# Attention with two heads in the two row halves of the matmul array, in units of a head pair and a query tile

## The reference

```python
def gqa_attend(q, k, v):
    s = einsum('bkgqd,bksd->bkgqs', q, k) * (HEAD_DIM ** -0.5)      # 1/8
    p = softmax(s, axis=-1)
    return einsum('bkgqs,bksd->bkgqd', p, v)
# latent queries (256) attend to context + latent keys (512); context queries (256) to context keys (256)
# q, k: RMS-normed over the 64 channels, the latent ones rotated; then y = o @ w_o for both streams
```

## Time and profile before

| what | value |
|---|---|
| time of three runs | 3343.28, 3342.68, 3339.27 us; median 3342.68 |
| profiled execution, span from first to last instruction | 3341.7 us (the profile gives no other time of that execution) |
| busy: TensorE matmul / weight loads | 3125.3 us (94%) / 2416.2 us (72%) |
| busy: VectorE / ScalarE / GpSimd | 1803.7 (54%) / 708.2 (21%) / 38.0 us (1%) |
| TensorE's mean granted clock | 0.973 |
| projections of the attention | about 2075 to 2160 us of the span |
| its units | 2160 to 2282 us |

### The profile page before, as it was taken

How to read it: one execution, slowest core, us unless ns; L and a number is a source line. 1 busy time by engine, 2 the same in 40 slices (tenths; PEclk the granted TensorE clock), 3 DMA queues, 4 the chain that set the end, 5 groups by cost and what they waited for, 6 DMA issues and landing times.

```text
span 3341.7 us, 50848 instructions
## 1 busy us (share of the span) xinstructions
PE 3125.3 (94%) x21694; PEld 2416.2 (72%) x21694; DVE 1803.7 (54%) x2751; ACT 708.2 (21%) x1342; POOL 38.0 (1%) x76
## 2 busy tenths in 40 slices
PE   8999988999998999999889998988999999998998
PEld 8987764558976997765457984544788886465797
DVE  5554554556555555454565555574434562287565
ACT  1112213212112102222311103261211001244110
POOL 1000000000000000000000000000000000000000
PEclk9999999999999999999999999999999999998999
DMA  8654402226655755321215743200223343231352
GB/s 272 227 173 140 164 28 76 76 76 218 213 185 184 252 172 173 128 88 65 88 51 183 236 150 132 76 1 26 76 76 101 114 163 107 77 125 58 127 177 101
DMA packets 279696, 430.75 MB, mean 129 GB/s; under 512 B 9880, under 2 KB 147456, under 8 KB 279472
## 3 DMA queue, kind: packets, MB, share of 16 engines
q1 hardware_dynamic: 273920, 411.52, 36.4%
q0 software_dynamic: 5088, 14.86, 1.4%
q10 hardware_dynamic: 464, 1.12, 0.1%
HBM read 426.43 MB, written 1.05 MB: 128 GB/s over the span
## 4 chain that ended last, share of the span: by engine, by line
PE 82%; DVE 11%; ACT 4%; issue 2%; DMA 1%; DVEq 0%; ACTq 0%; POOL 0%; SPq 0%; PEldq 0%
PE bank L446 80%; PE bank L449 2%; DVE arena L742 1%; ACT xT L993 1%; DVE arena L3700 1%; DVE arena L3621 1%; DVE arena L1761 1%; ACT xT L2810 1%; ACT arena L3137 0%; DMA ring<-in_ffn_w 0%; DVE stats L916 0%; DVE ctok L1773 0%; DMA ring<-in_ple_w_gate 0%; DVE arena L3268 0%; DVE ring L742 0%
## 5 line engine op out<-in xcount | busy, mean ns | idle before, releaser
L446 PE MATMUL bank<-arena 128*128 128x128 f32 (+8 forms) x7068 | 786.7, 286 | 49.9 <-DVEq L3704 8.4
L446 PE MATMUL bank<-xT,ring 128*128 128x128 f32 (+3 forms) x4640 | 808.5, 335 | 20.5 <-ACTq L2818 9.9
L446 PEld LDWEIGHTS bank<-arena 128*128 128x128 f32 (+3 forms) x7068 | 667.7, 164 | 165.9 <-issue 27.0
L446 PEld LDWEIGHTS bank<-xT,ring 128*128 128x128 f32 (+1 forms) x4640 | 691.9, 194 | 130.7 <-issue 55.0
L446 PE MATMUL bank<-ring,xT 128*128 128x512 f32 (+2 forms) x1408 | 592.2, 572 | 17.0 <-ACT xT L2810 8.7
L446 PEld LDWEIGHTS bank<-ring,xT 128*128 128x128 f32 x1408 | 261.2, 194 | 287.6 <-issue 268.7
L446 PE MATMUL bank<-ring,arena 128*128 128x256 f32 (+1 forms) x1584 | 448.5, 436 | 19.7 <-DVE arena L839 6.5
L446 PEld LDWEIGHTS bank<-ring,arena 128*128 128x128 f32 x1584 | 302.8, 193 | 140.2 <-issue 91.0
L782 DVE TENSOR_TENSOR arena<-arena,bank 128x256 f32<-128x256 f32 (+1 forms) x198 | 92.2, 466 | 427.1 <-PE bank L446 287.2
L694 ACT COPY arena<-bank 128x256 f32<-128x256 f32 (+1 forms) x264 | 107.8, 408 | 777.5 <-PE bank L446 776.5
L742 DVE TENSOR_TENSOR arena<-ring,arena 128x1024 f32<-128x1024 f32 (+1 forms) x216 | 257.1, 1190 | 7.4
(11 more groups left out here) (391 smaller groups left out, 2140.1 us busy)
## 6 DMA issues: line engine op xcount, KB each, us to landing
ring<-in_ffn_w SPq DMA_DIRECT2D x88, 1024.0 KB, 8.0
ring<-in_w_in SPq DMA_DIRECT2D x32, 2048.0 KB, 7.7
ring<-in_ffn_w_in SPq DMA_DIRECT2D x44, 1024.0 KB, 6.9
arena<-in_ada_w SPq DMA_DIRECT2D x18, 2048.0 KB, 13.6
ring<-in_ffn_w SPq DMA_DIRECT2D x16, 2048.0 KB, 7.9
ring<-in_ffn_w_out SPq DMA_DIRECT2D x12, 2048.0 KB, 8.2
ring<-in_hgrn_w_in SPq DMA_DIRECT2D x12, 2048.0 KB, 7.9
ring<-in_ffn_w SPq DMA_DIRECT2D x8, 1536.0 KB, 6.6
```

The source lines that it names most:

```text
L446: return self.e.matmul(o, lhsT, rhs, start=start, stop=stop, skip_group_check=True)
```

## The change

- Keys are kept once, as `kk` (each key head written twice side by side, one copy with a broadcast source) and `kT`, 4 x 512 columns instead of 8 x 512; there is no zeroed buffer. The upper and the lower 64 partitions of a column of `kT` hold the same key head. A tile's keys need four transposes and one copy.
- A score product runs over 64 partitions: `qT[r_, ...]` and `kT[r_, ...]` with `r_` the upper or lower half. The even head goes through the upper half of the array's rows into one bank, the odd head through the lower half into the next bank.
- A unit is a head pair and a query tile in the latent stream (16 units), and a head pair with both query tiles in the context stream (8 units).
- The banks of the units are fixed: scores in banks 4 and 5 or 6 and 7 by the unit's parity (`score_pair`), turned probabilities in 2 and 3 (`turn_pair`), weighed values in 0 or 1. All eight banks are now one tensor, so that one instruction can read two. New semaphores count units: scores_ready, scores_read, probs_turned, values_weighed, values_kept.
- A unit has one maximum over both banks (1024 columns) and one product with -0.125. The scalings of a unit are issued without a wait between them. The second copy of turned probabilities is VectorE's in the context stream.
- The order is TensorE scores(u), turn_probs(u-2), weigh(u-3); ScalarE keep_PT(u-2), exps(u); VectorE maxes(u), scale(u-1), keep_PT(u-2) (context), keep_o for unit u-4.

```diff
-        kz = t(8, P)
-        kTz = t(8, 512)
+        kk = t(4, P)
+        kT = t(4, 512)
...
-                for src in (qk_tok[:, QKV_ORDER[n - 1]], kz[:].rearrange("p a b -> p (a b)")):
-                    for q in range(2):
+                for src, nq in ((qk_tok[:, QKV_ORDER[n - 1]], 2), (kk[:].rearrange("p a b -> p (a b)"), 1)):
+                    for q in range(nq):
...
+            pe.wait_ge(to_act.freed, to_act.next_free() + 3)
+            pe.wait_ge(to_dve.freed, to_dve.next_free() + 3)
             def scores(u):
...
+                i, s, qt = units[u]
+                if u >= 2:
+                    pe.wait_ge(scores_read, u - 1)
+                for q in (qt,) if s == 0 else range(2):
+                    for par, r_ in enumerate(CHUNKS):
+                        bank = score_pair(u)[:, par]
+                        o = bank if s == 0 else bank[:, q * SEQ:(q + 1) * SEQ]
+                        mm = pe.mm(o, qT[r_, i, s * SEQ + q * P:s * SEQ + (q + 1) * P], kT[r_, i // 2, s * SEQ:512])
+                mm.then_inc(scores_ready, 1)
             def turn_probs(u):
...
+                pe.wait_ge(probs_scaled, u + 1)
+                if u:
+                    pe.wait_ge(PT_ready, 2 * u)
+                for par in range(2):
+                    for k in range(4):
+                        o = k * P if s == 0 else k % 2 * SEQ + k // 2 * P
+                        mm = pe.turn(turn_pair[:, par, k * P:(k + 1) * P], Pb[:, u % 2, par, o:o + P])
+                    mm.then_inc(probs_turned, 1)
+            def weigh(u):
+                n = 8 * s + i
+                bank = psum[n % 2]
+                pe.wait_ge(PT_ready, 2 * u + 2)
+                if n >= 2 and qt == 0:
+                    pe.wait_ge(values_kept, n - 1)
+                nk, w = (4, P) if s == 0 else (2, SEQ)
+                for k in range(nk):
+                    for par, r_ in enumerate(CHUNKS):
+                        mm = pe.mm(bank[r_, qt * P:qt * P + w], av_tok[:, 2 * s + k, g_], PT[:, u % 4, par, k * w:(k + 1) * w],
+                                   k == 0, k == nk - 1)
+                if s or qt:
+                    mm.then_inc(values_weighed, 1)
+            for u in range(len(units) + 3):
+                if u < len(units):
                     scores(u)
+                if 2 <= u < len(units) + 2:
+                    turn_probs(u - 2)
+                if u >= 3:
+                    weigh(u - 3)
...
         def attention_units():
-            return [(h, s) for s in range(2) for h in range(16)]
+            return [(i, 0, qt) for i in range(8) for qt in range(2)] + [(i, 1, 0) for i in range(8)]
...
             def exps(u):
+                if u >= 2:
+                    act.wait_ge(probs_turned, 2 * u - 2)
+                act.wait_ge(scores_ready, u + 1)
+                act.wait_ge(max_ready, act.due(max_ready))
+                for j in range(2 if s == 0 else 4):
+                    ins = e.activation(probs(u, j), src, ACT.Exp, scale=0.125, bias=bias[:, j:j + 1],
+                                       accum_out=total[:, j:j + 1])
...
+                ins.then_inc(scores_read, act.up(scores_read))
             def keep_PT(u):
+                for par in range(2 if units[u][1] == 0 else 1):
+                    act.wait_ge(probs_turned, 2 * u + par + 1)
+                    ins = e.copy(PT[:, u % 4, par], turn_pair[:, par])
...
+            for u in range(len(units) + 2):
+                if u >= 2:
+                    keep_PT(u - 2)
                 if u < len(units):
                     exps(u)
...
-            v.memset(kz[:], 0.0).then_inc(dve_step, dve.up(dve_step))
...
+                ins = v.tensor_copy(kk[:].rearrange("p g (r n) -> p g r n", r=2),
+                                    x[:, 16:20].unsqueeze(2).broadcast_to([P, 4, 2, 64]))
...
             def maxes(u):
+                dve.wait_ge(scores_ready, u + 1)
+                src = score_pair(u)
+                if units[u][1]:
+                    src = src.rearrange("p r (q n) -> p r q n", q=2)
+                ins = v.tensor_reduce(by_query(u, am[:, 16:24]), src, AX.X, ALU.max)
...
             def scale(u):
+                v.reciprocal(r, by_query(u, am[:, 8:16])).then_inc(dve_step, dve.up(dve_step))
+                dve.wait_ge(dve_step, dve.sent(dve_step))
+                for j in range(n):
+                    ins = v.tensor_scalar(probs(u, j), probs(u, j), r[:, j:j + 1], None, ALU.mult)
...
+            for u in range(len(units) + 4):
+                if u < len(units):
+                    maxes(u)
+                if 1 <= u <= len(units):
+                    scale(u - 1)
+                if u >= 2 and u - 2 < len(units) and units[u - 2][1]:
+                    keep_PT(u - 2)
+                if u >= 4:
+                    i, s, qt = units[u - 4]
+                    if s or qt:
+                        keep_o(8 * s + i)
```

More of the change, by code:

```diff
@@ L283, in two_blocks @@
         block_landed = [sem(f"block_landed{i}") for i in range(RING)]
-        psum = [ctx.enter_context(nc.psum_tensor(f"bank{i}", [P, 512], F32)) for i in range(8)]
+        bank_all = ctx.enter_context(nc.psum_tensor("bank", [P, 8, 512], F32))
+        psum = [bank_all[:, i] for i in range(8)]
         to_dve = Banks(psum[:4], dve_bank_filled, dve_bank_freed)
@@ L3029, in turn_probs @@
-            def turn_probs(u):
[L3030 to L3050, removed]
-                for k in range(nk):
[L3052 to L3056, removed]
@@ L3095, in act_attention @@
                     t0 = QKV_ORDER[n - 1] * P
-                    for dst in (qT, kTz):
-                        for q in range(2):
+                    for dst, nq in ((qT, 2), (kT, 1)):
+                        for q in range(nq):
                             act.wait_ge(to_act.filled, to_act.next_filled())
@@ L3118, in exps @@
             def exps(u):
[L3119 to L3144, removed]
-                            ins.then_inc(act_step, act.up(act_step))
-                            act.wait_ge(act_step, act.sent(act_step))
-                    act.sem_inc(probs_ready, act.up(probs_ready))
@@ L3149, in keep_PT @@
-            def keep_PT(u):
-                h, s = units[u]
-                for k0 in range(0, 4 if s == 0 else 2, 2):
-                    act.wait_ge(to_act.filled, to_act.next_filled())
-                    bank = to_act.filled_bank()
-                    ins = e.copy(PT[:, u % 4, k0:k0 + 2], bank[:].rearrange("p (k t) -> p k t", k=2))
-                    ins.then_inc(to_act.freed, act.up(to_act.freed))
-                    act.wait_ge(to_act.freed, act.sent(to_act.freed))
-                act.sem_inc(PT_ready, act.up(PT_ready))
@@ L3276, in keep_o @@
-            def keep_o(u):
-                h, s = units[u]
-                dve.wait_ge(to_dve.filled, to_dve.next_filled())
-                bank = to_dve.filled_bank()
-                ins = v.tensor_copy(oT[:, h // 2, s * SEQ:(s + 1) * SEQ], bank[:, 0:SEQ])
-                ins.then_inc(to_dve.freed, dve.up(to_dve.freed))
-                dve.wait_ge(to_dve.freed, dve.sent(to_dve.freed))
-            for u in range(len(units) + 3):
+                dve.wait_ge(scores_ready, u + 1)
+                src = score_pair(u)
@@ new lines, in scale @@
+            def scale(u):
+                r = by_query(u, am[:, 24:32])
+                dve.wait_ge(probs_ready, dve.due(probs_ready))
+                v.reciprocal(r, by_query(u, am[:, 8:16])).then_inc(dve_step, dve.up(dve_step))
+                dve.wait_ge(dve_step, dve.sent(dve_step))
+                n = 2 if units[u][1] == 0 else 4
+                for j in range(n):
+                    ins = v.tensor_scalar(probs(u, j), probs(u, j), r[:, j:j + 1], None, ALU.mult)
+                    done = probs_scaled if j == n - 1 else dve_step
+                    ins.then_inc(done, dve.up(done))
+                dve.wait_ge(dve_step, dve.sent(dve_step))
+                dve.wait_ge(probs_scaled, dve.sent(probs_scaled))
@@ L3285, in dve_attention @@
+            for u in range(len(units) + 4):
                 if u < len(units):
                     maxes(u)
-                if u >= 4 and u % 2 == 0:
-                    keep_o(u - 4)
-                if u < len(units):
-                    scale(u)
+                if 1 <= u <= len(units):
[6 more added lines that the diff above has]
+                        keep_o(8 * s + i)
```

120 lines of the change are left out of this document (46 added, 74 removed).

## The result

The changed kernel takes 3306.4 us (median of 4 runs) beside 3341.3 for the kernel before: ratio 0.9891, interval 0.9877 to 0.9905, 34.8 us less. In two later groups of runs it was 3313.3 (ratio 0.9920, 0.9903 to 0.9937) and 3308.0 (0.9900, 0.9883 to 0.9916). Beside the kernel before in the same groups that is 27.1 and 31.5 less, so the total tells the gain to some 8 us only, and what follows rests on the traces. I forecast 3313, some 30 less, with 3309 to 3317 as the forecast's own range.

The account below looks back on a forecast made before the run. TensorE was taken to bound the latent stream, VectorE the context stream. Projections -1.9 and attention -28.0 gave -29.9 us from 3342.68: 3312.8, forecast 3313, own range 3309 to 3317, wider range 3306 to 3325.

Parts of the forecast that it names:

- the wide one: Range of the total that leaves out rivals D, E and the edges: 3306 to 3325 us.
- Projections: Before the attention: 16 fewer key transposes and one fewer last copy on ScalarE, together -1.9 us.
- S: Score products of a latent unit on TensorE: 1.28 us, between 0.86 (full overlap) and 1.71 (none).
- Three slots, 1.28: Latent scores: in-order queue lets only second half A run beside first half B, so 1.28 us a unit.
- rival B: Latent scores overlap fully: S 0.86, a unit 3.07, -5 us, total 3308; chance 0.10.
- W: Weighing in a latent unit on TensorE: 16 instructions of 128 columns, 0.90 us.
- the changes of shape: TensorE's tile-shape switches in a latent unit: two more visible ones at 0.15 us each, between 0 and 0.24.
- T: Transposes in a latent unit on TensorE: eight, 1.01 us, unchanged in number.
- Start: Start of attention: table load under the first maximum, T0 at 6.2 us, 1.5 added for a lower clock.
- Context stream: Eight attention units bound by VectorE at 4.34 us each; entry 16.5, three periods 13.0, tail 9.8.
- Behind it: Output projection after attention: starts at the low clock before and after, weights no new wait; nothing added to the sum.
- Rival D: TensorE's clock stays at 1.2 GHz in the attention stage: latent +38 us, context +15, total 3366; chance 0.04.

Follow-up runs that it names:

- the one with zeros: Changed kernel's units, banks and order, but keys with zeros beside them and score products over all 128 rows: 3321.8 us, ratio 0.9942.
- the halves alone: Kernel before, its units, banks and order kept, but keys kept once and score products over 64 rows: 3347.7 us against 3339.7, ratio 1.0021.
- the two maxima: Changed kernel with two maxima of 512 columns a unit instead of one of 1024: 3310.0 us, ratio 0.9911.
- one unit ahead: Changed kernel, but transposes of unit u-1, weighing of u-2, and VectorE's scaling in the round of its maximum: 3352.5 us, ratio 1.0032.
- both products in one half: Changed kernel with both score products of a unit in the upper row half, the even head's computed twice: 3324.6 us, ratio 0.9955.

## Where the prediction was right, and where it failed

The direction, the stage and the engines that bound it held. The first group's 3306.4 lies below the forecast's own range of 3309 to 3317 and at the lower edge of the wide one. By the profiled spans the gain was 4.9 us larger than forecast: 4.4 from the latent rounds, 2.3 behind the stage and 0.7 ahead of the attention, less 1.5 in the context stream and 1.0 in the rest. The other two groups' gains, 27.1 and 31.5, lie on both sides of the 29.9; that these come nearer says nothing for the sum, since the stage in their traces, 91.9 and 91.6, is within 1 us of the first one's.

- **Projections**: -1.9 forecast. The trace has -2.6 up to the first scores, of which 0.7 was there before the first attention transposes (2080.68 before, 2079.98 after); -1.9 is left. The stretch from those transposes to the first scores repeats: 79.4 in the kernel before and in the one with zeros, 77.4 in all three profiles of the changed kernel and with the halves alone.
- **The step that failed is S.** I wrote "Three slots, 1.28". It measured 0.86: rival B, to which I gave 0.10, was the case, and with it 3308 against 3306.4 measured. The first context scores come 50.1 us after the first scores (first row below), where I had 54.5; the twelve rounds before them take 3.12 on average instead of 3.50, and that is the 4.4. The argument for three slots was an in-order queue that no row of the trace had shown; one product half beside the next, and even one after four of the other, overlap in full. The burst on 64 x 64 tiles already ran near the full four-fold rate (1.10 us with its tail, where the columns need 0.86), and I should have given it more weight. The section of the Trainium skill that I had set beside the rows (TensorE: Matmul & The Clock Gate, "Measured speedup vs the span model") says that packed tiles finish in about one matmul. The trace agrees with that rule: 0.86 and not 1.28.

```profile
2207.57 0.73 PEld L452 LDWEIGHTS bank<-arena 64*128 64x128 f32 x8 [0.17 <-issue]
...
2224.87 1.23 DVE L3234 TENSOR_REDUCE arena<-bank 128x4 f32<-128x1024 f32 x1
...
2237.49 1.22 DVE L3234 TENSOR_REDUCE arena<-bank 128x4 f32<-128x1024 f32 x1
...
2244.03 1.06 PE L455 MATMUL bank<-cst,arena 128*128 128x128 f32 x8 [0.67 <-DVEq L3258]
...
2246.61 1.08 PE L452 MATMUL bank<-arena 128*64 128x256 f32 x8 [0.50 <-DVE arena L3262]
```

- **ScalarE** was sized at 2.95 a latent unit and measures 3.19: the two copies take 1.28 together, and 0.20 passes between a copy and the next exp. With TensorE down to 3.10, that became the bound of the last units, so a little of S's error was given back.
- **W** (0.90) and the changes of shape (0.15 each): T, W and S with all switches were to be 3.49; with S at 0.86 that is 3.07, and 3.10 was measured.
- **Start**: the table load does not lie under the first maximum; the load waits until the maximum is there (2160.18), and the first transposes came at 6.9 instead of 6.2. The clock of a stretch of 6 us there was 0.72, as in the kernel before.
- **Context stream**: period 4.34 forecast, 4.20 measured, because the four scalings without waits take 1.14 (1.23 to the next instruction) and not 1.45. Its entry and tail were mis-sized the other way. By the rows above, the entry to the fifth maximum took 17.3 (16.5 forecast), three periods 12.6 (13.0) and the tail 10.9 (9.8): 1.5 longer in all. In the tail I had left out that the last transposes wait for VectorE's copy of turned probabilities of the unit before, and the last weighing for its copy of weighed values (last two rows). VectorE as bound is confirmed by the two maxima (+0.19 a unit gave +0.20) and by moving work away from it.
- **Behind it** I had put nothing, since I took the projection to start at the low clock before and after. It starts at 0.65 in the one profile of the kernel before and at full clock in every profile of this document's other kernels, with the halves alone too, in the old units and order. So the -2.3 is measured, but that the change brings it is not shown.
- **Rival D** did not happen in this kernel, but its mechanism is real and fits what makes the halves alone slower than before. I had argued against it from a burst of half-array products without a wait, and from waits between full-array products; the case that counts has both.

Left open: why the changed kernel's single runs spread from 3300.6 to 3322.0, when those of the kernel before spread from 3335.1 to 3344.6. In the one profile at 3322 the stage is as in the others (91.6), and most of the loss lies in the recurrent layer some 650 us later, whose code is the same: that profile lags the first one by 2.7 us where the layer begins (2892 us) and by 12.9 where it ends (3078 us). The granted clock there is 0.87 (first row, the run at 3322) against 0.94 (second row, the first profile of the changed kernel):

```profile
2901.50:3081.50 180.00, 160.15 (x1075) 106.91 (x1074) 135.10 (x134) 68.14 (x93) 0.53 (x1) 0.87 0.21 74
```

```profile
2900.00:3080.00 180.00, 154.20 (x1089) 98.52 (x1088) 141.07 (x144) 67.94 (x94) 0.54 (x1) 0.94 0.25 85
```

## What to carry to other kernels

Two half-height products in the two row halves cost what one costs, if a unit of work holds both; products of one half alone cost the same as full ones and can pull the clock down. When a round trip between three engines is longer than any engine's own work, the lead in the issue order can be worth more than the cheaper instruction: here the order and the units brought 19 us of 31, and in the old order, one unit ahead, the whole change was slower than nothing. After that, TensorE (3.10) and ScalarE (3.19) were within 3% of each other in the latent stream, so a further move has to be checked on every engine, and its gain in the stage's tail too.

## What the runs showed that I had not expected

- Half-array scores in waiting units: granted clock 0.72 over 67 us, where full-array ones with zeros had 0.96, and 0.55 in a stretch of 11 us in which TensorE was busy throughout. With both products in one half, 0.57 over the first 12 us, 10.5 of them busy.
- Four instructions to one row half followed by four to the other take 1.14 us, as with the halves in turn (1.13).
- One more change of tile shape a unit, between scores and transposes, went with 0.15 us more (3.96 against 3.81).
- Four scalings of 128 x 256 without waits between take 1.14 us, 0.29 each, where one alone takes 0.35.
